# Where the operands of the matmuls begin in the on-chip memory, and the order of three small jobs on TensorE

## What is computed

```python
h = rms_norm(x, norm_g)
proj = h @ w_in                      # 1024 -> 8704 columns: 68 tiles of 128
u_ssm, z_ssm, q, k, v, z_attn, q_mem, z_mem, gate_logits = split(proj)
y = gelu(s5_ssm(u_ssm, ...))
o_ssm = y * sigmoid(y @ w_glu + b_glu) * silu(z_ssm)
o_attn = merge(dilated_window_attention(q, k, v) for 3 dilations) * silu(z_attn)
o_mem = softmax(q_mem @ k_mem.T / sqrt(128)) @ v_mem * silu(z_mem)
merged = sum(sigmoid(gate_b) * (o_b @ w_br_b) for b in the 3 branches)
out = rms_norm(x + merged @ w_out, final_norm_g)
```

## The kernel before

| tensor | role in the large matmuls | address before | modulo 512 | modulo 2048 |
|---|---|---|---|---|
| w_hi | weights | 12416 | 128 | 128 |
| w_lo | weights | 20608 | 128 | 128 |
| wx_hi | weights, stage 4 | 62976 | 0 | 1536 |
| wx_lo | weights, stage 4 | 71168 | 0 | 1536 |
| h_hi | moving, stage 2 | 38400 | 0 | 1536 |
| h_lo | moving, stage 2 | 103936 | 0 | 1536 |
| ys_hi, ys_lo | moving, stage 3 | 62976, 112128 | 0 | 1536 |
| o_hi, o_lo | moving, stage 4 | 79360, 112128 | 0 | 1536 |
| m_hi, m_lo | moving, stage 4 | 157184, 173568 | 0 | 1536 |

## Time and profile before

### The profile page before, as it was taken

How to read it: one execution, slowest core, us unless ns; L and a number is a source line. 1 busy time by engine, 2 the same in 40 slices (tenths; PEclk the granted TensorE clock), 3 DMA queues, 4 the chain that set the end, 5 groups by cost and what they waited for, 6 DMA issues and landing times. The chain is left out here.

```text
span 2682.1 us, 30604 instructions
## 1 busy us (share of the span) xinstructions
PE 2572.4 (96%) x12062; PEld 2068.1 (77%) x12062; DVE 1432.1 (53%) x2547; ACT 594.4 (22%) x1251; POOL 190.5 (7%) x330
## 2 busy tenths in 40 slices
PE   6899999999999999999999999999969699999997
PEld 4588888888888888887777777888847488888885
DVE  6517768676743343413444443354226567777775
ACT  4312122222211111112333343323242102020201
POOL 0000000000001111110000000011100000000000
PEclk8899999999999999999999999999989799999998
DMA  5122343433344555551323343477444575748471
GB/s 174 63 99 93 97 134 124 136 113 120 116 145 159 165 175 174 177 179 57 118 83 106 110 138 125 150 224 238 136 172 153 173 230 151 253 152 257 155 222 55
DMA packets 180947, 395.66 MB, mean 148 GB/s; under 512 B 26559, under 2 KB 68643, under 8 KB 174916
## 3 DMA queue, kind: packets, MB, share of 16 engines
q1 hardware_dynamic: 145652, 253.14, 30.9%
q0 software_dynamic: 35152, 140.55, 14.8%
HBM read 252.72 MB, written 140.88 MB: 147 GB/s over the span
## 5 line engine op out<-in xcount | busy, mean ns | idle before, releaser
L136 PE MATMUL bank<-h_hi,w_hi 128*128 128x512 f32 (+1 forms) x2208 | 906.2, 410 | 18.9 <-DVE w_lo L130 18.3
L138 PE MATMUL bank<-h_hi,w_lo 128*128 128x512 f32 (+1 forms) x2208 | 869.8, 394 | 0.0
L137 PE MATMUL bank<-h_lo,w_hi 128*128 128x512 f32 (+1 forms) x2208 | 869.0, 394 | 0.0
L136 PEld LDWEIGHTS bank<-h_hi,w_hi 128*128 128x128 f32 x2208 | 417.8, 189 | 127.0 <-issue 23.9
L138 PEld LDWEIGHTS bank<-h_hi,w_lo 128*128 128x128 f32 x2208 | 417.0, 189 | 96.2
L137 PEld LDWEIGHTS bank<-h_lo,w_hi 128*128 128x128 f32 x2208 | 417.9, 189 | 91.2 <-issue 1.7
L128 DVE CAST w_hi<-w_raw 128x1024 fp32r<-128x1024 f32 (+1 forms) x130 | 89.5, 688 | 326.7 <-PE bank L138 246.7
L130 DVE TENSOR_TENSOR w_lo<-w_raw,w_hi 128x1024 fp32r<-128x1024 f32 (+1 forms) x130 | 157.7, 1213 | 4.5
L634 POOL DMA_DIRECT2D proj_d<-ev x160 | 87.8, 549 | 987.9 <-ACT ev L767 608.5
L1169 DVE COPY ptr<-bank 128x512 f32<-128x512 f32 x80 | 51.5, 686 | 187.7 <-PE bank L1442 187.7
L1105 DVE TENSOR_TENSOR tv<-bank,csb 128x512 f32<-128x512 f32 x48 | 33.2, 692 | 219.7 <-PE bank L1373 219.7
(11 more groups left out here) (242 smaller groups left out, 3395.4 us busy)
## 6 DMA issues: line engine op xcount, KB each, us to landing
proj_d<-ev POOLq DMA_DIRECT2D x160, 256.0 KB, 3.3
w_raw<-w_in SPq DMA_DIRECT2D x68, 512.0 KB, 5.0
gt<-proj_d POOLq DMA_DIRECT2D x32, 768.0 KB, 8.0
proj_d<-ev POOLq DMA_DIRECT2D x22, 1024.0 KB, 4.2
w_raw<-w_br SPq DMA_DIRECT2D x32, 512.0 KB, 4.7
space<-w_br SPq DMA_DIRECT2D x32, 512.0 KB, 4.7
mats<-mats_d SPq DMA_DIRECT2D x48, 320.0 KB
space<-o_d SPq DMA_DIRECT2D x14, 1024.0 KB, 7.5
```

Of the source, the lines that this page charges most:

```text
L136: nc.tensor.matmul(out, ah, bh, start=(start and n == 0), stop=False)
L137: nc.tensor.matmul(out, ah, bl, start=False, stop=False)
L138: last = nc.tensor.matmul(out, al, bh, start=False, stop=(stop and n == len(pairs) - 1))
```

## The change

Two edits. In the first the tensors that live through the whole kernel are made in another order, ident and the small ones first, and a tensor of 512 bytes that nothing uses, `to_2048`, is put behind them. In the second `turn` stands ahead of `output` in TensorE's `side_beat`.

```diff
-        w_raw = sb(ctx, "w_raw", [P, 2, KD, P])
-        w_hi = sb(ctx, "w_hi", [P, 2, KD, P], F32R)
-        w_lo = sb(ctx, "w_lo", [P, 2, KD, P], F32R)
-        k_mem = sb(ctx, "k_mem", [P, MH, ML])
-        v_mem = sb(ctx, "v_mem", [P, 2, MH * MD])
         ones = sb(ctx, "ones", [P, P])
+        ident = sb(ctx, "ident", [P, P])
         g_in = sb(ctx, "g_in", [P, 3, KD])
         bg = sb(ctx, "bg", [P, 24])
         bgh = sb(ctx, "bgh", [P, 24])
         bglu = sb(ctx, "bglu", [P, KS])
         eps = sb(ctx, "eps", [P, 1])
-        ident = sb(ctx, "ident", [P, P])
         sign = sb(ctx, "sign", [P, 1])
+        w_hi = sb(ctx, "w_hi", [P, 2, KD, P], F32R)
+        w_lo = sb(ctx, "w_lo", [P, 2, KD, P], F32R)
+        w_raw = sb(ctx, "w_raw", [P, 2, KD, P])
+        k_mem = sb(ctx, "k_mem", [P, MH, ML])
+        v_mem = sb(ctx, "v_mem", [P, 2, MH * MD])
+        to_2048 = sb(ctx, "to_2048", [P, 128])
...
                     def side_beat(beat):
+                        t = turn_at(beat)
+                        if t is not None:
+                            turn(t)
                         t = step_at(beat, 5)
                         if t is not None:
                             output(t)
-                        t = turn_at(beat)
-                        if t is not None:
-                            turn(t)
                         t = step_at(beat, 0)
                         if t is not None:
                             scores(t)
```

## The result

The changed kernel takes 2644.82 us (median of four executions, 2639.41 to 2645.86) against 2680.57 us for the kernel before in the same series (2679.03 to 2683.07). The ratio is 0.9862, with a 95% interval of 0.9845 to 0.9879. The forecast was 2631 us. A second series of the changed kernel gave a median of 2640.75 us in four executions against 2682.50, ratio 0.9845 (0.9831 to 0.9858). Over all series three executions were disturbed (5365, 5415 and 3246 us); every comparison leaves them out.

The account below looks back on a forecast made before the run. TensorE's matmul count times start-to-start distance was taken as the bound. Less 45.1 us for w's place, less 3.7 for the order, plus 0.2 for a wait: 2679.6 - 48.6 = 2631 us, 8 in 10 for 2618 to 2650.

Parts of the forecast that it names:

- What bounds the kernel: TensorE has a matmul in flight for 2572.4 of 2682.1 us; time is matmul count times start-to-start distance.
- The price of a w matmul: 512-column matmuls reading w would go from 232.5 to 226.9 ns; 8050 x 5.6 ns = 45.1 us less.
- Weights to a multiple of 512: w would begin at 1536 modulo 2048, as wx does, and so take its distance; bounds 0 and 5.6 ns a matmul.
- The third rival: Weights' and moving operand's remainders must match within 2048; w matmuls would get slower: 2736 us, halfway 2706; chance 0.07.
- The moving operands: Starting 512-column moving operands at a multiple of 2048 avoids a crossing; taken as 0, at most 13.6 ns a matmul gained.
- The order: Attention beats with turn before output save one operand-shape change, 0.1 us in 38 steps: 3.7 us less (0 to 7.4).
- The query wait: TensorE's 1.47 us wait for the memory branch's first queries would grow by 0.2 us, to 1.7.
- Sum: Less 45.1, less 3.7, plus 0.2: 48.6 us less, from a median of 2679.6 to 2631 us.
- No address effect: The gap between w and wx comes from something other than address, so only the reordering pays: 2676 us; chance 0.08.
- the crossing counts: Crossing a multiple of 2048 costs 13.6 ns; w matmuls alone would save 109 us, about 2520 us; chance 0.07.

Follow-up runs that it names:

- experiment 9: Changed kernel with the two state-space side jobs in one place after each chunk's second half, 24 projection matmuls between visits: 2641.00 us, ratio 0.9842.
- experiment 10: On top of experiment 9, the memory branch's scores, transposes and output in one beat instead of two: 2635.84 us, ratio 0.9828.
- Experiment 7: Changed kernel with w, h, ys, o and m all at 128 modulo 512 and wx at 0: 2646.16 us, one execution.
- experiment 2: Kernel before with only `to_2048` added behind `sign`: w stays at 128 modulo 512, wx and moving operands at 0 modulo 2048; 2681.99 us, ratio 0.9997.
- experiment 4: Changed kernel without `to_2048`, so moving operands stay at 1536 modulo 2048: 2640.17 us, ratio 0.9841.
- experiment 6: Changed kernel with moving operands h at 128 and m at 256 modulo 512; w, wx, ys and o at 0: 2667.89 us, one execution.
- experiment 3: Kernel before with `turn` ahead of `output` and nothing else: 2676.27 us, ratio 0.9979, 5.75 us less.
- experiment 8: The changed kernel again, unaltered, in a later series: 2638.27 to 2643.65 us, ratio 0.9845.
- experiment 1: Changed kernel without `to_2048` and with the old order of side jobs, so only the weights moved: 2648.32 and 2648.87 us, ratio 0.9873.
- experiment 11: Changed kernel with w at 192 and wx at 32 modulo 512, moving operands at 0: 2659.59 us, one execution.

## Why the prediction was right, and where it was wrong

*What bounds the kernel.* Right. TensorE's distance sets the time; no other engine became late. The median of 2644.82 us lies within the range for 8 in 10 (2618 to 2650) and 0.8 us above the range given for the forecast itself (2624 to 2644); 35.8 us were gained in that series where 48.6 were forecast.

*The price of a w matmul.* Right for steady flow: 226.7 ns where 226.9 was forecast. The sum made of it was too large. The mean distances of the traces (those under 260 ns) fell by 4.3 ns for the 6528 matmuls of h (232.5 to 228.2), by 5.4 for 432 of ys, 5.7 for 768 of o and 5.7 for 384 of m: 28.1 + 2.3 + 4.4 + 2.2 = 37.0 us instead of 45.1. The step that failed is "I take the wx distance for every 512-column matmul that reads w". It carried a distance from long units into a stage where a side job cuts the flow mostly every 12 to 36 matmuls; experiments 9 and 10 show that each visit costs the fast pair 0.02 to 0.05 us until its distance is steady: 3.2 us less around the state-space stretch with half the visits. In the stretch from the last transpose of the tables to the first attention scores the excess over 226.7 ns is 8.0 us before and still 4.1 us after.

*The cause of that price.* Named wrongly: "Weights to a multiple of 512". Experiment 7 shows weights at 0 that are slow and weights at 128 that are fast. The third rival had the right kind of cause, the distance between the two remainders, with the wrong modulus: 256, not 2048. The argument against it, that tiles take all four steps of 512 while a unit is even, was sound against 2048 and silent on 256, since 512 is a multiple of 256. Both readings gave the same time for this change because it leaves every pair at a difference of 0: that the number held under the wrong cause is luck, since all moving operands happened to begin at a multiple of 512. The remark in that rival that the pair w and h is "slow in either role" in 256 columns had no fast pair to be compared with, and the changed kernel's 120.0 ns contradict it.

*The moving operands.* Right: 0 for their place modulo 2048, by experiments 2 and 4; their place modulo 256 counts as much as that of the weights (experiment 6). The working has one slip that changes nothing: from 256 to 512 columns the excess of the w pair grows by 19.2 - 11.9 = 7.3 ns, not by "about 6.5 to 7", and it compared pairs whose dependence on the address turned out opposite. What remains above one column per cycle, 226.7 - 213.3 = 13.4 ns, isn't explained by any run.

*The order.* The mechanism was right, the size too small: 5.75 us in experiment 3, 0.15 us a beat, where 0.10 was taken. The change from 64 columns to 64 rows costs one change, as taken; that the transposes themselves run 0.06 us longer behind the output's narrow weights was put down to "such an extra at its end" for all jobs alike and not counted as something that goes. The room in front of the transposes shrank from 2.0 to 0.7 us, a little more than forecast (0.9), and it held. In one of the four tightest steps the last exponential of the changed kernel is read at

```profile
1589.38 0.18 ACT L808 ACTIVATION_READ_ACCUMULATOR tsc<-tsc,stat 128x1 f32 x1
```

and the transposes start at

```profile
1590.28 1.03 PE L1443 MATMUL bank<-ident,tsc 128*128 128x128 f32 x8
```

0.7 us later, and no wait appeared.

*The query wait.* 1.48 us, as before, instead of 1.7: 0.2 us off, of no weight.

*Sum.* 37.0 + 5.7 = 42.7 us of the forecast's 48.6. The medians say 35.8 in the first series and 41.8 in each of the two later ones (experiment 4, without the pad, against 2682.02, and experiment 8 against 2682.50). The first series gave less, by an amount that executions of one kernel differ by; what sets it stays open. The traces place part of it at the start and part in the last stage (537.5 to 543.0 us for the same code). *No address effect* is out by experiment 1, *the crossing counts* by experiment 2.

## What to carry to other kernels

Where TensorE flows without waits, measure the distance from one matmul's start to the next for each pair of operand tensors; if it differs, shift one of the two tensors and look again. For 512 columns of fp32r the two should begin at the same place modulo 256 bytes, which is worth 2.4% of the steady distance here; for 256 columns the same place was the slowest of those seen, so measure at the width that you use. Before such a gain is multiplied by the number of matmuls, look how long the flow runs between two interruptions: a steady distance has to be reached again after each, so small jobs are better put together.

## What the runs showed of the hardware

- The distance of 512-column fp32r matmuls depends on the difference between the start of the weights and that of the moving operand, modulo 256 bytes: 226.7 ns at 0, 233 at 32 and 64, 232.5 at 128, 229.2 at 192. It isn't symmetric (64 above costs 6.6 ns, 64 below 2.5), and no second address effect at 2048 was seen (ratio 0.9997).
- With 256 columns the order is another: 120.0 ns at a difference of 0, 118.5 at 128, 113.3 at 64 (experiment 11, w moving).
- The slow distances are means of a repeating row. By the single starts in the trace of before they alternate between 229 and 237 ns or go 232, 231, 232, 229, 230, 232, 241 and again; at 192 they go 226, 229, 232. The fast pair is steady at 226 or 227.
- The fast distance isn't there at once. Behind a job of another shape four to nine distances between 224 and 236 ns come first, for the most part the end of one and the same row, entered at a place that depends on the job. In these first distances the fast pair is only about 1 ns faster than the slow one (eleven distances in 2.53 us against 2.54), so the state-space stretch got only 8 matmuls in 1307 from the change.
- Going from full-width weights to 64 columns costs TensorE about 0.10 us at the boundary, so does going back, and so does going from 64 columns to 64 rows; full transposes behind the narrow job pay another 0.06 us behind their first matmul. With the narrow jobs side by side a beat has three such boundaries instead of four.
